# Token-tiled output products at the ends of two hybrid layers

## What is computed

```
def first_block(x, ...):
    for l in range(DEPTH):                       # DEPTH = 2
        h = rms_norm(x, norm_g[l])
        ... three branches y_a, y_b, y_c from h @ w_in[l] ...
        branches = jnp.stack([y_a, y_b, y_c], axis=2)
        proj = jnp.einsum("bsnw,nwd->bsnd", branches, w_branch_out[l])
        gates = jax.nn.sigmoid(jnp.einsum("bsd,dne->bsne", h, w_gate[l]))
        merged = jnp.sum(gates * proj, axis=2)
        x = x + merged @ w_out[l]
    return rms_norm(x, final_norm_g)
```

## Time and profile before

| what | us |
|---|---|
| median of 3 runs | 1894.14 |
| lowest and highest | 1891.67 and 1897.22 |
| the profiled execution's own time | 1895.27 |
| its span | 1893.5 |
| PE busy | 1771.0 (94%) |
| DVE busy | 1150.7 (61%) |
| ACT busy | 893.4 (47%) |

### The profile page before, as it was taken

How to read it: one execution, slowest core, us unless ns; L and a number is a source line. 1 busy time by engine, 2 the same in 40 slices (tenths; PEclk the granted TensorE clock), 3 DMA queues, 4 the chain that set the end, 5 groups by cost and what they waited for, 6 DMA issues and landing times. The chain is left out here.

```text
span 1893.5 us, 24635 instructions
## 1 busy us (share of the span) xinstructions
PE 1771.0 (94%) x10424; PEld 1462.7 (77%) x10424; DVE 1150.7 (61%) x1555; ACT 893.4 (47%) x1088; POOL 12.3 (1%) x26
## 2 busy tenths in 40 slices
PE   7899899898998997999999998999999999779998
PEld 5787688777877885888887776888878887668886
DVE  4676876557768856555567445655565556775554
ACT  4453534354444442444464545644464445645443
POOL 0000000000000000000000000000000000000000
PEclk9899999998999998999999998999999999979999
DMA  6231345441214453455553222555555555335543
GB/s 260 89 113 49 138 156 190 154 168 67 91 68 150 171 200 135 160 184 190 208 189 112 89 89 89 193 203 196 178 192 208 189 181 195 124 111 210 179 178 111
DMA packets 41470, 291.76 MB, mean 154 GB/s; under 512 B 4640, under 2 KB 4768, under 8 KB 7184
## 3 DMA queue, kind: packets, MB, share of 16 engines
q1 hardware_dynamic: 38720, 280.16, 41.2%
q0 software_dynamic: 2640, 10.03, 1.5%
HBM read 289.12 MB, written 1.05 MB: 153 GB/s over the span
## 5 line engine op out<-in xcount | busy, mean ns | idle before, releaser
L458 PE MATMUL pg<-wh,hTh 128*128 128x512 f32 (+1 forms) x2160 | 855.3, 396 | 42.2 <-DVE wl L1576 11.4
L1576 DVE TENSOR_TENSOR wl<-raw,wh 128x2048 fp32r<-128x2048 f32 x266 | 607.8, 2291 | 463.4 <-ACT wh L1121 462.5
L459 PE MATMUL pg<-wl,hTh 128*128 128x512 f32 (+1 forms) x2160 | 837.0, 387 | 0.0
L460 PE MATMUL pg<-wh,hTl 128*128 128x512 f32 (+1 forms) x2160 | 836.7, 387 | 0.0
L1121 ACT ACTIVATE wh<-raw 128x2048 fp32r<-128x2048 f32 x266 | 507.8, 1913 | 452.7 <-PE pg L460 444.5
L458 PEld LDWEIGHTS pg<-wh,hTh 128*128 128x128 f32 x2160 | 411.9, 191 | 140.0 <-issue 43.0
L460 PEld LDWEIGHTS pg<-wh,hTl 128*128 128x128 f32 x2160 | 411.1, 190 | 82.7
L459 PEld LDWEIGHTS pg<-wl,hTh 128*128 128x128 f32 x2160 | 412.2, 191 | 75.4
L1200 ACT ACTIVATE arena<-pg,sm 128x512 f32<-128x512 f32 (+1 forms) x47 | 31.4, 669 | 142.2 <-PE pg L460 142.1
L718 PEld LDWEIGHTS ps<-arena 64*64 64x64 f32 x1792 | 54.0, 135 | 11.8 <-issue 5.0
L718 PE MATMUL ps<-arena 64*64 64x64 f32 x1792 | 57.0, 220 | 4.0 <-DVE arena L1773 2.1
(11 more groups left out here) (347 smaller groups left out, 1190.8 us busy)
## 6 DMA issues: line engine op xcount, KB each, us to landing
raw<-weights SPq DMA_DIRECT2D x266, 1024.0 KB, 4.8
arena<-wide POOLq DMA_DIRECT2D x9, 512.0 KB, 3.6
x<-x_in SPq DMA_DIRECT2D x1, 1024.0 KB, 5.0
cst<-const_tables POOLq DMA_DIRECT2D x1, 1024.0 KB, 5.1
plainh<-dist_tables POOLq DMA_DIRECT2D x2, 512.0 KB, 4.8
arena<-gate_mix POOLq DMA_DIRECT2D x1, 1024.0 KB, 7.8
arena<-token_mix POOLq DMA_DIRECT2D x2, 256.0 KB, 3.7
y_out<-x POOLq DMA_DIRECT2D x1, 512.0 KB, 2.9
```

The costliest lines, as they stand in the source:

```text
L458: pe.matmul(dst, lh, rh, start=first, stop=False)
L459: pe.matmul(dst, lh, rl, start=False, stop=False)
L460: return pe.matmul(dst, ll, rh, start=False, stop=last)
L1576: tt(wl[:, slot, :], raw[:, u % RAW_SLOTS, :], wh[:, slot, :], ALU.subtract)\
```

## The change

Three things are rewritten on PE, ACT and DVE alike.

1. The first half of the merged output is transposed inside the last branch unit, after two of its four chunks; the second half inside the first unit of the output product, after three of its four chunks. They go to chunks 12 to 19 of `hTh`/`hTl` and no longer to 0 to 7.
2. The output product's second block runs tile after tile. After layer 0 (`next_layer_x`) the first half of x is transposed for both tiles during tile 0 (`first_halves`), tile 0's second half during tile 1 (`first_tile_rest`), and tile 1's second half within the next layer's first block, which now runs tile after tile too (`head=l > 0, first_at=(2,)`).
3. After layer 1 (`first_norm`) the same block runs tile after tile. The final norm uses `next_x` with `sums=True`: ACT sums the squares of x and takes the root, DVE adds, multiplies by the gain and scales each tile. The next feed-forward layer starts with tile 0.

```diff
-    for n in range(3): ...
-        gemm(BW, (512,) * 2, ("evac_dve",) * 2, chunk0=16 - 4 * n)
-    c.wait("y_ready")
-    transpose_groups(merged, (0, 1), 0)
-    gemm(D, (512,) * 2, ("evac_dve",) * 2, between=second_half, after=1)
+        gemm(BW, (512,) * 2, ("evac_dve",) * 2, chunk0=16 - 4 * n,
+             inside=(1, 1, merged_half(0)) if n == 2 else None)
+    last_layer = l == DEPTH - 1
+    gemm(D, (512,) * 2, ("evac_dve",) * 2, chunk0=MERGED_AT, inside=(0, 2, merged_half(1)),
+         tail=first_tile(X_AT) if last_layer else first_tile_rest, early=None if last_layer else first_halves)
...
 (PE)
+            def first_halves(n):
+                if n in (2, 4):
+                    c.wait("x_ready")
+                    tile_groups(n // 2 - 1, 0, 0)
+            def first_tile_rest(n):
+                if n == 2:
+                    c.wait("x_ready")
+                    tile_groups(0, 0, 1)
...
 (ACT)
-                transpose_split(KD, 0)
-                gemm(D, (512,) * 2, ("evac_dve",) * 2)
+                split_groups((0, 1), MERGED_AT)
+                pump(st.used + 3)
+                split_groups((2, 3), MERGED_AT)
+            def next_layer_x(gain):
+                st.used += 2
+                pump(st.used + 2)
+                for m in range(M):
+                    tile_split(m, gain, 0, 0)
+                st.used += 2
+                pump(st.used + 1)
+                ...
+                tile_squares(0, True)
+                c.wait("tile_done")
+                tile_split(0, gain, 0, 1)
+                pump(st.used + 2)
+                tile_split(1, gain, 0, 1)
+                pump(st.used + 3)
+                tile_squares(1, True)
...
 (DVE)
+            def add(b, m):
+                pair = 2 * ((st.block + b) % 2)
+                o = slice(512 * b, 512 * b + 512)
+                return tt(x[:, m, o], x[:, m, o], pg[:, pair + m, :], ALU.add)
...
+            def tile_update(m, half, sums):
+                if sums:
+                    c.sig(add(1, m), "x_sum")
+                    ...
+                    c.step(tt(XN[:, m, 512:D], x[:, m, 512:D], G[:, 512:D], ALU.mult))
+                    c.wait("product_sq")
```

More of the change, by code:

```diff
@@ L500, in products, with tile_after_tile @@
                                      wh[:, slot, i * w:(i + 1) * w], wl[:, slot, i * w:(i + 1) * w], start, stop)
-            def tile_after_tile(pair, w, units, begin, end, between, during, done=None):
+            def tile_after_tile(pair, w, units, begin, end, between, during, done=None, both=None):
                 first = st.used
@@ L851, in merge_out, with merged_half, between @@
                 gemm(D, (512,), ("evac_act",))
+                merged = V(0, 2048).rearrange("p (m d) -> p m d", m=M)
+                def merged_half(b):
+                    def between():
+                        c.wait("y_ready")
+                        transpose_groups(merged, (2 * b, 2 * b + 1), MERGED_AT)
+                    return between
                 for n in range(3):
@@ L1330, in merge_out, with first_norm @@
                 gemm(BW, (512,) * 2, ("evac_dve",) * 2)
-                transpose_split(KD, 0)
-                gemm(D, (512,) * 2, ("evac_dve",) * 2)
+                split_groups((0, 1), MERGED_AT)
[8 more added lines that the diff above has]
+                pump(st.used + 1)
+                st.evacs["evac_dve"] += 2
+                st.block += 2
+                tile_squares(0, True)
[5 more added lines that the diff above has]
+                tile_squares(1, True)
+                c.wait("rs_ready")
+            def first_norm(gain, dst):
+                st.used += 2
+                pump(st.used + 2)
+                for m in range(M):
+                    c.wait("x_sum")
+                    c.sig(act.activation(V(2048, 512), x[:, m, 0:512], ACT.Square, accum_out=SS4[:, m:m + 1]),
+                          "product_sq")
+                st.used += 2
+                pump(st.used + 1)
+                st.evacs["evac_dve"] += 2
+                st.block += 2
+                next_x(gain, dst, sums=True)
             def product_squares(i, pair):
@@ L1412, in gains, with ffn @@
                 return lambda k: name[:, k:k + 1]
[L1414 to L1416 removed]
+            def ffn():
                 hid = V(0, 2 * FF).rearrange("p (m f) -> p m f", m=M)
@@ new lines, in first_norm @@
+            def first_norm(gain, dst):
+                st.used += 2
+                pump(st.used + 2)
+                dve.wait_ge(sem["unit_used"], st.used)
+                for m in range(M):
+                    c.sig(add(0, m), "x_sum")
+                c.sig(dve.engine_nop(), "evac_dve")
+                dve.wait_ge(sem["final_g_landed"], 16)
+                for m in range(M):
+                    tt(XN[:, m, 0:512], x[:, m, 0:512], G[:, 0:512], ALU.mult)
+                c.wait("product_sq", 2)
+                c.sig(ts(SB, SS4[:, 0:2], 1.0 / D, EPS, ALU.mult, ALU.add), "sb_ready")
+                c.step(ts(SBH, SB, -0.5, None, ALU.mult))
+                st.used += 2
+                pump(st.used + 1)
+                next_x(1.0, gain, dst, sums=True)
@@ L2066, in next_x @@
                 dve.wait_ge(sem["unit_used"], st.used)
-                tile_update(1, half)
+                tile_update(1, half, sums)
+                if sums:
+                    st.evacs["evac_dve"] += 2
+                    st.block += 2
                 if gain is not None:
```

182 lines of the change are left out of this document (102 added, 80 removed).

## The result

The changed kernel takes 1880.8 us (median of 4 runs, 1879.44 to 1882.65) against 1894.1 for the kernel before; the ratio is 0.9922, 95% interval 0.9908 to 0.9936. The forecast was 1883.5 in a range of 1878 to 1889.5. The profiled execution took 1882.65 (span 1880.9, granted clock 0.973, before 0.967). The same kernel taken again later gave 1884.15 with a ratio of 0.9951 (0.9936 to 0.9966), so the gain is 9 to 13 us.

What follows compares the result with a forecast made beforehand. TensorE was busy 94% of the span, so only its idle or slow places could win: merges 0, layer seam 2.45, last seam 8.2, together 10.6 us off the 1894.14 median, giving 1883.5; range 1878 to 1889.5.

Steps and rivals of the forecast that it cites:

- Point 1 and 2: Both layers' merges: transposes moved inside units gain 0 for each layer; bounds 1.1 gained, 1.2 lost.
- The chain of 5.63 us: Merge gap: ScalarE's and VectorE's queued work from last branch matmul's slot to restart starts later but stays as long.
- Point 3: Seam between the layers: new waits of 1.85 and 1.1 plus 4 x 0.45, 4.75 against 7.2, gain 2.45 us.
- Point 4: Seam into the second block: 4.9 us without matmul work against 13.1, gain 8.2; bounds 10.2 and 3.3.
- + 0.39: Last seam: wait before the second tile's first matmul, counted as 0.39 us as in the recurrent mixer's output product.
- the twin: Recurrent mixer's output product at 1685, already handed over tile by tile; waits 0.53, 0.20 and 0.39, clock 1.00.
- A: Rival: the clock falls in the seams' new waits, costing 1.7 to 2.5 us each; 1887.7 or 1889.8; chance 0.17.
- B: Rival: weight units come late at the seams, each losing 1 to 3 us; 1888 to 1889; chance 0.08.
- C: Rival: both merge gaps close, 2 x (4.59 + 1.07 + 2.5) us more gained; 1867; chance 0.04.
- D: Rival: gaps close together hold 1.2 GHz through the seams; 18 us lost, 10.6 gained, 1901.5; chance 0.05.
- 1.6 to spare: Last seam: ScalarE's table load for the root, 1.28 us, would end at 5.8, 1.6 us before the square.

Runs made afterwards that it cites:

- e3_after_again: The changed kernel once more, unedited: 1884.15 us, ratio 0.9951 to the kernel before.
- e6_seam_order: Changed kernel with VectorE's tile steps in both seams before the weight unit's subtraction, and in the last seam ScalarE's tile 0 squares behind tile 1's splits: 1881.89 us.
- e5_splits_first: Changed kernel with the first half's low parts on VectorE before the second half's merge steps, and the weight unit split behind both on the two engines: 1867.76 us.
- e7_both_orders: Changed kernel with the edits of e5_splits_first and e6_seam_order together: 1864.12 us, ratio 0.9842 to the kernel before.

## Why the prediction held, and where it did not

**Point 1 and 2, the merges: mechanism right, size short by 0.1 to 0.9 each.** The chain of 5.63 us was forecast from the earlier trace rows and came out at 5.63; a gap of 5.5 to 5.9 was forecast and 5.47 came; the wait of 1.07 went. I took 0 for each and measured 0.69 and 0.93, and 0.88 and 0.06 in e3_after_again. The larger term behind it is the slow stretch, which I had kept at 2.5 us: in the first trace 10 matmuls are slow behind the gap of layer 0 and 9 behind that of layer 1, and before the change it was 12 each. That is worth 0.4 and 0.6, and no row let me foresee it; in the second layer of e3_after_again it was 13, and the gain there shrank to 0.06. The other term is that the two insertions of 8 transposes cost 0.96 and 0.88 us, together 1.84, where I had counted 1.1 and 1.03 and the kernel before lost 2.19 at its second set: 0.3 gained each.

**Point 3, the seam between the layers: right in each term.** Counted in slots (the time from one matmul's start to the next one's, less 0.227), as the forecast was, with 0.09 for the long matmul behind and less the 0.45 that the transposes cost anyway, the two waits are 2.21 + 0.09 - 0.45 = 1.85 (forecast 1.85) and 1.48 + 0.09 - 0.45 = 1.12 (1.1). The profile's own idle, 1.64 and 0.91, is smaller by the modelled tail of the matmul before. Gain 2.38, forecast 2.45. The cause, DVE's subtraction for a weight unit ahead of the tile's add, is shown by e6_seam_order, where that order alone was changed in this seam and both waits went.

**Point 4, the last seam: forecast 8.2, measured 6.45.** In the same counting the waits are 0.97, 0.76, 1.23 and 1.85, where I had 1.05, 0.6, 1.05 and 0.39. The step that failed is the last, "+ 0.39", taken over from the twin. ACT's timeline of the changed kernel:

```profile
753.49 0.30 ACT L1444 ACTIVATE sm<-sm 128x1 f32<-128x1 f32 x1
753.69 1.90 ACT L1141 ACTIVATE wh<-raw 128x2048 fp32r<-128x2048 f32 x1
755.49 0.62 ACT L1430 ACTIVATE xn<-x 128x512 f32<-128x512 f32 x1
...
756.23 0.63 ACT L1430 ACTIVATE xn<-x 128x512 f32<-128x512 f32 x1
...
756.98 2.17 ACT L1421 ACTIVATE hTh<-ps,par 128x128 fp32r<-128x128 f32 x8
```

Behind the root ACT owes a weight unit and two squares, 3.5 us, before it copies the transposes. In the twin they were over when the transposes came (1702.85), because there the transposes came 3.9 us after that root; here they came 1.5 after it, at 755.00. I had followed DVE's chain to x and not ACT's queue to the split. In e6_seam_order, with tile 0's squares put behind the splits, the excess is 0.69 + 0.11 - 0.45 = 0.35, near the twin's 0.39, and the whole wait of 1.59 is gone from the timeline. That run also changed DVE's order here; that the squares made this wait is read from ACT's timeline, where the splits follow them without a pause, and not from a run of its own.

**The sum** was 10.6; where the code changed it is 10.45. That they agree so closely is luck: I had 1.6 too little at the merges and 1.75 too much at the last seam, and the two errors cancel. The rest up to 12.6 is in code that the change does not touch. A forecast for the median could hardly have had it.

**The rivals.** A, a slow clock in the new waits: no, the windows read 1.00 over waits of 1.64 and 1.59. B, late weight units: no such wait stands in the seams; the segments behind them (71.45 and 71.43 us before the gates of layer 1, 127.05 and 127.06 after the last seam) are unchanged. C, the merge gaps close: not here, but its price was right: I had 16.3 us more for the two merges, and in e5_splits_first, which closes them, they take 16.9 less than before. Its total of 1867.8 against my 1867 agrees also because the unedited hybrid was 2.0 us shorter in its trace. D, the clock held down through the seams: no, 1.00.

**Smaller terms.** The adds of 128x512 took 0.68 us and the gain products 0.69, as counted, and they did not set the sum. Two instructions of 0.69 take more than one of 128x1024, which took 1.22; that fits the rule of a fixed latency per instruction in the Trainium skill, page "VectorE: DVE Perf Modes", section on the TRN2 errata. The table load for the root, in ACT's timeline of the changed kernel:

```profile
739.90 1.28 ACT L1451 ACT_TABLE_LOAD   x1
...
742.99 0.64 ACT L1443 ACTIVATE arena<-x 128x512 f32<-128x512 f32 x1 [1.59 <-DVE x L2055]
```

It took 1.28 us, and ACT then waited 1.59 for x, as forecast (1.6 to spare). The Trainium skill, page "ScalarE: Activation LUTs", rules for kernel authors, wants about 2.7 us budgeted for a switch; this trace shows less than half of it, for ACT's next instruction began at 741.20, right behind the load.

## What to carry over

Moving TensorE's transposes ahead gave little here (0.1 to 0.9 us a merge) while the engines that must take them up had something else first in their queues: list for each engine what stands between the result and its use, weight units above all, and move that too. A wait taken from a twin holds only if every queue in it is as far along; check it for each engine, not just for the longest chain. And read a gain of a few us by segments of equal work, for the unedited rest can move by as much.

## What the runs showed of the chip

The granted clock in unedited code is not a constant of that code. The hybrid mixer's segment took 231.8 to 239.3 us over 14 traces with the same instructions, layer 1's 241.6 to 243.3, while segments at the full clock (400.0 to 400.1 for the 1766 matmuls behind the hybrid, 127.05 to 127.07 behind the last seam) repeat to 0.1. With nearly the same seam before it (26.25 to 26.55) it took 237.44 to 237.59 in four traces, and 235.01 and 235.90 in the two of the changed kernel (28.49 and 28.48); with a seam longer than 26.25 by 1.2 and 4.7 us it took 239.3 and 233.4, in one trace each. What moves it is not shown. Of useless transposes in the seam's waits, 8 cost nothing and 16 cost 0.3 us. So edits worth 4.9 us in the seams of e6_seam_order showed nothing in the total (1881.9 and 1881.6 against 1880.8 and 1884.2), and in the trace of e7_both_orders the hybrid was 3.2 us shorter than in the first trace of the changed kernel.
